# A decoder step with a 32-expert layer: overflow-table places moved into the expert loop, first experts' TensorE work reordered, weight loads released later

## What is computed

```python
def hier_moe(x, ...):
    g_idx = argmax(xf @ w_rg + b_rg)            # one of 4 groups
    e_sel = (xf @ w_re + b_re)[:, g_idx]        # 8 experts of that group
    top_v, top_i = lax.top_k(e_sel, 2)
    top_w = softmax(top_v) * g_gate
    # 32 experts: hid = silu(x @ w_e1) * (x @ w_e3) * gate;  y += hid @ w_e2
x = x + hier_moe(rmsnorm(x, g_ffn), ...)
y = rmsnorm(x, g_final)
```

## Time and profile before

| | us |
|---|---|
| three runs | 1177.85, 1183.08, 1186.43 (median 1183.08) |
| profiled execution | 1186.26, its span 1184.4 |
| mean granted TensorE clock in it | 0.946 of full speed |
| PE busy | 1077.7 (91%) |
| DVE busy | 626.4 (53%) |
| ACT busy | 431.9 (36%) |
| POOL busy | 195.6 (17%) |

### The profile page before, as it was taken

How to read it: one execution, slowest core, us unless ns; L and a number is a source line. 1 busy time by engine, 2 the same in 40 slices (tenths; PEclk the granted TensorE clock), 3 DMA queues, 4 the chain that set the end, 5 groups by cost and what they waited for, 6 DMA issues and landing times. The chain is left out here.

```text
span 1184.4 us, 13950 instructions
## 1 busy us (share of the span) xinstructions
PE 1077.7 (91%) x5251; PEld 853.1 (72%) x5251; DVE 626.4 (53%) x1186; ACT 431.9 (36%) x755; POOL 195.6 (17%) x144
## 2 busy tenths in 40 slices
PE   3999999899999999998775999967999999999966
PEld 2899998797886469995542778855677777777722
DVE  5824644226644200004564114677988888888627
ACT  4522111205312011212322102244677777777513
POOL 3401121000000102200000300204432222332100
PEclk9999999898999999999797899976999999999978
DMA  9501111225001641107206201149999999999275
GB/s 331 140 19 36 40 54 36 89 72 208 1 1 62 190 139 37 54 1 284 108 0 248 72 1 54 72 169 351 328 396 381 382 393 379 387 388 367 107 291 191
DMA packets 55017, 203.02 MB, mean 171 GB/s; under 512 B 10534, under 2 KB 19231, under 8 KB 41383
## 3 DMA queue, kind: packets, MB, share of 16 engines
q1 hardware_dynamic: 44167, 181.61, 41.7%
q0 software_dynamic: 10784, 20.52, 4.7%
HBM read 189.52 MB, written 28.36 MB: 184 GB/s over the span
## 5 line engine op out<-in xcount | busy, mean ns | idle before, releaser
L476 PE MATMUL bank<-regA_r,regW_r 128*128 128x352 f32 (+1 forms) x456 | 149.5, 328 | 0.0
L475 PE MATMUL bank<-regA_r,regW_r 128*128 128x352 f32 (+1 forms) x456 | 149.3, 327 | 0.0
L474 PE MATMUL bank<-expert_w_r,regS_r 128*128 128x512 f32 x256 | 105.5, 412 | 2.6 <-DVE regS_r L2037 2.6
L327 POOL TENSOR_TENSOR regW_r<-regW,regW_r 128x1024 fp32r<-128x1024 f32 x19 | 45.9, 2421 | 318.0 <-ACT regW_r L321 318.0
L1366 ACT ACTIVATE regY_r<-expert_w 128x1024 fp32r<-128x1024 f32 x88 | 91.6, 1062 | 2.8 <-DMA expert_w<-in_we 2.8
L474 PE MATMUL bank<-regY_r,regW_r 128*128 128x352 f32 (+1 forms) x264 | 88.0, 333 | 0.5 <-ACT regB L1108 0.5
L2020 DVE TENSOR_TENSOR expert_w_r<-expert_w,regY_r 128x1024 fp32r<-128x1024 f32 x69 | 82.8, 1219 | 7.6 <-ACT regY_r L1366 7.6
L475 PEld LDWEIGHTS bank<-regA_r,regW_r 128*128 128x128 f32 x456 | 86.5, 190 | 0.4
L476 PEld LDWEIGHTS bank<-regA_r,regW_r 128*128 128x128 f32 x456 | 86.0, 189 | 0.0
L475 PE MATMUL bank<-regY_r,regB_r 128*128 128x512 f32 (+1 forms) x216 | 85.9, 398 | 0.0
L476 PE MATMUL bank<-regY_r,regA_r 128*128 128x512 f32 (+1 forms) x216 | 85.8, 397 | 0.0
(11 more groups left out here) (314 smaller groups left out, 2300.6 us busy)
## 6 DMA issues: line engine op xcount, KB each, us to landing
expert_w<-in_we SPq DMA_DIRECT2D x96, 1024.0 KB, 7.8
regW<-in_wbc SPq DMA_DIRECT2D x11, 512.0 KB, 3.6
regA<-in_kct SPq DMA_DIRECT2D x5, 1024.0 KB, 6.9
regY<-in_cache_mem_v SPq DMA_DIRECT2D x5, 1024.0 KB, 8.3
regS<-in_x_prompt SPq DMA_DIRECT2D x8, 512.0 KB, 9.0
regY<-in_xt SPq DMA_DIRECT2D x8, 512.0 KB, 8.5
regX<-in_x_prompt SPq DMA_DIRECT2D x8, 512.0 KB, 6.5
regW<-in_wq SPq DMA_DIRECT2D x8, 512.0 KB, 3.7
```

Of the source, the lines that this page charges most:

```text
L327: eng.tensor_tensor(lo, raw, hi.bitcast(F32), ALU.subtract).then_inc(w_lo[name], 1)
L474: nc.tensor.matmul(out, stays[0], moves[1], start=first, stop=False)
L475: nc.tensor.matmul(out, stays[1], moves[0], start=False, stop=False)
L476: ins = nc.tensor.matmul(out, stays[0], moves[0], start=False, stop=last)
```

## The change

The places of the overflow table are computed by DVE at the end of the turns e = 3, 4 and 5 of the expert loop, and the 18 table writes are issued by POOL two per turn at e = 8 to 16. Their work buffers move out of `regS`, which the expert loop uses, into `small` and `lgm`. On the PE `tokens(2)` stands behind `ab(1)`, and `tokens(3)` behind `yy(0)`. SP issues the weight loads from 4 on behind the third gather (`m_g[0]` at 32) and the second, no longer behind the first and the second.

```diff
--- before.py
+++ after.py
@@ -214,11 +214,10 @@
             chunk(("XB", k), "g", (*Yp, 512 * k), (regYr, 4 * N + 512 * k), 512)
 
         RM12 = v3(regS, 0, 2 * NT, NE)
-        EX = v3(regS, 1184, NT, 2)
+        EX = v3(small, 4, NT, 2)
         rank_of = v3(regS, 1216, 2 * GT, NE)
-        ranks_of = [regS[:, 3300 + 2 * GT * k:3300 + 2 * GT * (k + 1)] for k in range(NT // GT)]
-        rq, ra, rb, rc = (regS[:, 1420 + 2 * GT * k:1420 + 2 * GT * (k + 1)] for k in range(4))
-        ri = regS[:, 1460:1460 + 2 * GT]
+        ranks_of = [small[:, 24 + 2 * GT * k:24 + 2 * GT * (k + 1)] for k in range(NT // GT)]
+        rq, ra, rb, rc, ri = (lgm[:, 2 * GT * k:2 * GT * (k + 1)] for k in range(5))
         gix = regS[:, 1470:1470 + GT]
         gone = v3(regS, 1480, GT, NG)
         own = v3(regS, 1500, GT, NE)
@@ -878,9 +877,13 @@
                 ab(e)
                 if e == 0:
                     tokens(1)
-                if e + 2 < NE:
-                    tokens(e + 2)
-                if e >= 1:
+                elif e == 1:
+                    tokens(2)
+                    yy(0)
+                    tokens(3)
+                else:
+                    if e + 2 < NE:
+                        tokens(e + 2)
                     yy(e - 1)
                 hidden(e)
             yy(NE - 1)
@@ -1067,8 +1070,8 @@
             normed_store(NT - 1)
             for p in range(2, 4):
                 part_load(p)
-            for s in range(2):
-                sp.wait_ge(m_g[s], 16)
+            sp.wait_ge(m_g[1], 16)
+            sp.wait_ge(m_g[0], 32)
             for p in range(4, 3 * NE):
                 part_load(p)
             used(sp, ("down", NE - 1, 1))
@@ -1939,8 +1942,6 @@
                     route(t // GT - 1)
                 if t in (4, 7):
                     place(t // GT - 1)
-                if t == 4:
-                    place_in_table(0)
             add_bias(NT - 2)
             rstd(3, NT - 1)
             nc.vector.sem_inc(s_last, 1)
@@ -1955,8 +1956,6 @@
             link(tt(token_f, place_f, ps[:, 0:NE], ALU.add))
             nc.vector.tensor_copy(idx3[:, :, 0], token_f).then_inc(s_idx, 1)
             tt(idx3[:, :, 1], token_f, ps[:, 2 * NE:3 * NE], ALU.add).then_inc(sg, 1)
-            place_in_table(1)
-            place_in_table(2)
             tp = top[:, :].rearrange("p (t c) -> p t c", c=16)
             lg3 = lgm[:, :].rearrange("p (t c) -> p t c", c=LG)
             tt(gate[:, 0:NT], tp[:, :, 9], tp[:, :, 8], ALU.subtract)
@@ -2076,6 +2075,8 @@
                     spill_list()
                 if e == 2:
                     gates()
+                if 3 <= e < 3 + NT // GT:
+                    place_in_table(e - 3)
             y_right(NE - 1)
             dve.wait_ge(o_go, 1)
             n_spill = dve.value_load(spx[0:1, 16:17], min_val=0, max_val=SPILL)
@@ -2199,10 +2200,6 @@
                     bounds_check=P * NPLACE - 1, oob_is_err=False).then_inc(s_scat, 16)
 
             last_token, last_row = g.to_reg(N - 1), g.to_reg(2 * N - 1)
-            g.wait_ge(s_plc, 1)
-            for t in range(GT):
-                for c in range(2):
-                    place_rows(t, c)
             g.wait_ge(s_xnd[0], 16 * 5)
             g.wait_ge(s_xnd[1], 16 * 4)
             g.wait_ge(s_idx, 1)
@@ -2238,16 +2235,15 @@
             rows_in(1)
             rows_in(2)
             rows_in(3)
-            for t in range(GT, NT):
-                if t % GT == 0:
-                    g.wait_ge(s_plc, t // GT + 1)
-                for c in range(2):
-                    place_rows(t, c)
             for e in range(NE):
                 if e + 4 < NE:
                     rows_in(e + 4)
                 if e >= 1:
                     rows_out(e - 1)
+                if 8 <= e < 8 + NT:
+                    g.wait_ge(s_plc, (e - 8) // GT + 1)
+                    for c in range(2):
+                        place_rows(e - 8, c)
             rows_out(NE - 1)
             for s in range(2):
                 g.wait_ge(m_sc[s], 16 * (NE // 2))
```

## The result

The changed kernel takes 1188.04 us (median of 20 runs, 1183.57 to 1191.75) against 1181.96 for the kernel before in the same comparison (20 runs): ratio 1.0051, 95% interval 1.0037 to 1.0065, that is 4.4 to 7.7 us slower (6.1 between the medians). Forecast were 5.2 us more and 1188.3 us. The profiled execution took 1187.79 us, its span is 1185.8.

A forecast was written before the change was run, and what follows sets the result against it. PE was taken to set the pace of the steady loop, waiting only in the routing stage and at the loop start. Terms -2.6 - 0.9 + 8.7 = +5.2 us gave a forecast of 1188.3 us, range 1179 to 1197.

The forecast's parts named there:

- part C: Loop start, new PE order: token_lo(2) and the DVE work queued behind it delay hidden(1); cost 8.7 us.
- part B: Loop start: two place computations leave DVE there, so ab(0) can begin 1.24 us earlier; gain 0.9 us.
- Part A: Routing stage: the first place computation leaves DVE, PE's 1.08 us router wait and the clock dip go; gain 2.6 us.
- first rival: Loop start: the new PE order costs nothing, leaving only gains of 3.5 us, 1179.6 us; chance 0.17.
- Part D: Turns 3 to 5: DVE's place computations are hidden by hid's 2.9 us lead over PE; cost 0.
- if the cover were gone: Turns 3 to 5: without hid's lead the place computations would cost 3 x 1.7 = 5.1 us.
- Part E: Turns 8 to 16: two table writes per turn fit in POOL's 6.9 us of idle time; cost 0.
- third rival: Turns 8 to 16: the table writes make the DMA rings the bound, costing 23.4 us, 1211.7 us; chance 0.05.
- Part F: Weight loads from 4 on behind the third gather: load 4 just fits before ACT needs it; cost 0, at most 4 us.
- second rival: Loop start and routing: ab(1) and ab(2) wholly in low clock, routing dip stays; +11.9 us, 1195.0 us; chance 0.14.
- The fourth: Loop start: load 4 lands late for its first reader, ACT's part_to_hi; 1192.3 us; chance 0.06.

The follow-up runs named there:

- the order alone: The kernel before with only the new PE order (tokens(2) behind ab(1), tokens(3) behind yy(0)): 1191.15 us, ratio 1.0061.
- everything but the order: The changed kernel with the PE order of the kernel before, all else as changed: 1176.01 us, ratio 0.9943.
- the 6.1 us block: The changed kernel with spill_list moved whole from turn 0 to the end of turn 6, in buffers the loop does not use: 1185.02 us, ratio 1.0037.
- the run with the Silu table: The changed kernel with the old PE order, spill_list in six pieces in turns 6 to 11, and ACT's Silu table loaded early: 1171.41 us, ratio 0.9900.

## Why the prediction was right

**The sum and its sign** stand: +5.2 forecast, 4.4 to 7.7 measured, 4.7 in the edited places of the trace. That it is so near is partly luck. Against the trace, part C was 1.1 us too high at hidden(2) and part B 0.9 too large there, and the two errors nearly cancel. The 1188.3 us are as near because the base of three runs (1183.08) lay 1.1 us above the 1181.96 of twenty.

**Part A** (-2.6): 2.9 in the changed kernel; 3.0 again when it alone was undone. The low clock behind the gap went with the gap, as assumed, and came back with it.

**Part B** (-0.9): right on average at tokens(1), mis-sized behind it. ab(0) starts 0.7 us earlier instead of 1.24, since the first gather, called untouched, is slower beside the up_lo that now run next to its issue. After that the low clock of ab(0) varies: in the ten traces with this edit tokens(1) starts 15.39 to 16.66 us after the cast, 16.0 in the mean, against 17.0 in the three without it. At hidden(2) the gain is 1.7 and 2.1 us in the two runs that have the old order and no further edit, one execution each, and nothing in the changed kernel (55.61 us against 55.63 with the order alone, where ab(2) ran at full clock after its wait). This term takes part in making "everything but the order" faster than the -3.5 of the first rival; 2.0 us of its -6.7 stand in no row and lie inside its interval.

**Part C** (+8.7): in the order-alone run hidden(1) came 9.2 us later, and hidden(2) 7.6. The chain was the named one: token_hi(2), then token_lo(2) after 8.27 us of idle DVE, then all that is queued behind it. Of the 9.4 us between the changed kernel and the old order with the same rest (55.6 and 46.2 to hidden(2)), 5.4 went when the lists followed with PE's order unchanged. With spill_list gone from behind token_lo(2) as well, 0.9 are left (44.4 and 43.5). tokens(3) alone cost nothing. PE's wait in front of hidden(1) was 2.74 us, not the 4 that was to be seen, since yy(0) took longer in low clock.

**Part D** (0): the cost is shown by the trace, the working is not quite. hid(4) on DVE, pushed back by the first place computation, ends at 864.74, still 1.9 us ahead of hidden(4) on PE:

```profile
864.32 0.42 DVE L2040 TENSOR_TENSOR regW<-regY,bank 128x256 f32<-128x256 f32 x1
```

```profile
866.62 0.38 PE L827 MATMUL bank<-cst,regW 128*128 128x128 f32 x2
```

The lead was 2.93 us in the kernel before, so the first computation costs it 1.04 us; with the second and third it stays at 1.89, and behind them it is 2.93 again. DVE does not fall back further from turn to turn, as the 0.3 per turn of the prediction had it. That 1 us came out in sum is luck. The price "if the cover were gone" became real for the 6.1 us block: 3.9 us.

**Part E** (0): two table writes per turn, 1.96 and 0.98 us on POOL, fit. The third rival, DMA rings as the bound, falls: with the writes the DMA share is 1.01 and a write takes 7.1 us to land in the median, but PE stays busy in 93.00 of 93.00 us, the turn stays 9.67 us, and ACT waits for no load in this stretch. The 3.1 us of the earlier trace rows, from which the prediction priced this rival, take in six direct writes from the start of the kernel (1.8 us); the 18 indirect ones alone took 5.1 in the median, and the rival's price by its own rule would have been 9 x (5.1 - 0.5) = 41 us. What the Trainium skill says of transfers under 512 B (DMA: Bandwidth & Descriptors, Specifications) may hold for the writes themselves; no run here shows it in the time.

**Part F** (0): the third gather landed in 3.9 us, from 9.3 in the earlier trace rows, and with the loads released as before the time did not move beyond its interval. With the old PE order the release point was not tried by itself. There ACT once waited 1.53 us for a load in turn 1 in the run with everything but the order, and 1.1 us in the run with the Silu table, but no wait of PE follows from it: in the first hid(1) stood behind spill_list, and in the second PE waits for nothing from hidden(0) on.

**Rivals.** The first (the order is free) fell by the order-alone run. The second, low clock for all of ab(1) and ab(2), did not come: both recovered on the way, as they had before (from hidden(0) to the next tokens 8.3 us, before 8.2; from hidden(1) 7.2, before 7.4), though yy(0) ran in low clock, which no part had named. What the second rival quotes on the low clock as the default stands in the Trainium skill (TensorE: Matmul & The Clock Gate) under What's actually happening. Nor does each longer gap bring more of it here: behind 3.12 us of idle PE in the order-alone run ab(2) ran at full clock (5.8 us to the next tokens), behind 2.74 us in the changed kernel it did not (7.2). The fourth did not occur: with the loads released as before the time is the same.

## What to carry to other kernels

When a step of one engine's list is moved, find in each other engine's list the step that waits for it, and count all that is queued behind that step: here 0.8 us of transposes moved by one place cost 8 us, because the lists of ACT and DVE did not move with them. In the changed kernel 12.4 us of DVE's list, half of it spill_list, stood between the start of the waiting step and hid(1). Work that is moved into a full loop is free while it is less than what the engine has idle in that turn and its lead together. Count from the trace how much that is: here 3.6 us of a block of 6.1 were hidden, not the 1.44 + 2.9 that averages promise. What goes beyond is paid, with slow matmuls on top, so move it in pieces.

## What the runs showed that was not expected

- The issue of a gather on POOL took 1.52 and 1.88 us beside the long up_lo of DVE, which have two inputs in SBUF, and 1.00 beside an idle DVE. The Trainium skill (SBUF — State Buffer, SBUF: two separate sides) says that DVE and GpSimd share a port pair that is held for a whole instruction, and that a DVE operation with two inputs in SBUF takes it only against a GpSimd operation that reads SBUF. Issues longer by 0.5 and 0.9 us, each less than one up_lo (1.2 us), agree with such a hold; that it is the cause, and that issuing a gather reads SBUF in this sense, no run here shows.
- Executions differ ahead of any edit. The router matmul of tile 4, up to which all these kernels run the same instructions, starts between 745.1 and 752.3 us in the traces (746.81 in the run with the rest only, 752.13 in the one with the routing edit undone). That is more than most effects here, so a single span tells little, and distances between two points of one trace tell much. Even these carry the clock: cast to tokens(1) varies by 1.3 us over the same instructions.
- Removing 4.2 us of waiting in front of hidden(1) moved hidden(2) by 2.7 us: with TensorE's two clock levels the same 24 matmuls took from 5.5 us to about 8 in these traces. What sets the moment at which the clock rises, these runs do not show.
